# Two-block transformer kernel: up and gate tiles in pairs as seven block products of 256 tokens, and the down projection in chunks of four tiles between them

## The reference

```
first block:   h2 = rms_norm(x, norm_mlp)
               x  = x + square(relu(h2 @ w_up)) @ w_down          # 1024 -> 4096 -> 1024
second block, 2 layers, each with two of these around its mixer:
               h  = rms_norm(x, norm)
               x  = x + 0.5 * ((silu(h @ w_gate) * (h @ w_up)) @ w_down)   # 1024 -> 2816 -> 1024
out = rms_norm(x, final_norm)
```

## Time and profile before

| | |
|---|---|
| median of 3 runs | 2491.19 us |
| profiled execution | span 2488.4 us, PE busy 2471.6 us (99%) |
| DVE, ACT, POOL busy | 1235.0, 961.9, 198.7 us |
| matmuls | 11236 |

### The profile page before, as it was taken

How to read it: one execution, slowest core, us unless ns; L and a number is a source line. 1 busy time by engine, 2 the same in 40 slices (tenths; PEclk the granted TensorE clock), 3 DMA queues, 4 the chain that set the end, 5 groups by cost and what they waited for, 6 DMA issues and landing times.

```text
span 2488.4 us, 27808 instructions
## 1 busy us (share of the span) xinstructions
PE 2471.6 (99%) x11236; PEld 2046.0 (82%) x11236; DVE 1235.0 (50%) x1674; ACT 961.9 (39%) x1415; POOL 198.7 (8%) x207
## 2 busy tenths in 40 slices
PE   9999999999999999999999999999999999999999
PEld 7878888888888888888888888888888888888887
DVE  7742554434474343466554444643444665544443
ACT  6677343322443232357432222422222575322223
POOL 2231010000020000012200000100000122000001
PEclk9999999999999999999999999999999999999999
DMA  7655433333233333245433332333332364333332
GB/s 212 141 129 124 136 102 103 95 100 101 85 94 101 102 93 95 86 134 143 119 94 102 93 101 86 102 95 100 93 102 81 123 142 129 94 102 93 102 91 79
DMA packets 79279, 267.40 MB, mean 107 GB/s; under 512 B 9904, under 2 KB 13232, under 8 KB 78768
## 3 DMA queue, kind: packets, MB, share of 16 engines
q1 hardware_dynamic: 69376, 233.57, 31.0%
q0 software_dynamic: 9776, 32.06, 6.4%
HBM read 234.56 MB, written 2.19 MB: 95 GB/s over the span
## 4 chain that ended last, share of the span: by engine, by line
PE 90%; DVE 3%; issue 2%; ACT 2%; POOL 1%; DMA 1%; SPq 0%; POOLq 0%; DVEq 0%; ACTq 0%
PE bank L845 29%; PE bank L847 29%; PE bank L846 29%; DVE w_lo L1237 1%; PE bank L861 1%; PE bank L876 1%; ACT w_hi L1006 1%; DVE x L1367 1%; PE bank L899 1%; ACT z L994 0%; PE bank L888 0%; PE bank L889 0%; ACT h_hi L1019 0%; POOL rel_bias L1561 0%; POOL square_sum L1542 0%
## 5 line engine op out<-in xcount | busy, mean ns | idle before, releaser
L845 PE MATMUL bank<-h_hi,w_hi 128*128 128x512 f32 x2224 | 872.4, 392 | 3.6 <-DVE w_lo L1237 1.5
L846 PE MATMUL bank<-h_lo,w_hi 128*128 128x512 f32 x2224 | 866.6, 390 | 0.0
L847 PE MATMUL bank<-h_hi,w_lo 128*128 128x512 f32 x2224 | 866.4, 390 | 0.0
L1237 DVE TENSOR_TENSOR w_lo<-w_raw,w_hi 128x1024 fp32r<-128x1024 f32 (+2 forms) x392 | 484.0, 1236 | 289.8 <-ACT w_hi L1006 288.6
L1006 ACT ACTIVATE w_hi<-w_raw 128x1024 fp32r<-128x1024 f32 (+1 forms) x435 | 449.1, 1034 | 398.7 <-PE bank L847 396.5
L845 PEld LDWEIGHTS bank<-h_hi,w_hi 128*128 128x128 f32 x2224 | 417.7, 188 | 88.0 <-DVE h_lo L1252 2.7
L847 PEld LDWEIGHTS bank<-h_hi,w_lo 128*128 128x128 f32 x2224 | 417.5, 188 | 88.0
L846 PEld LDWEIGHTS bank<-h_lo,w_hi 128*128 128x128 f32 x2224 | 417.9, 188 | 81.9 <-issue 0.5
L845 PE MATMUL bank<-act_hi,w_hi 128*128 128x512 f32 x960 | 373.6, 389 | 0.0
L846 PE MATMUL bank<-act_lo,w_hi 128*128 128x512 f32 x960 | 373.6, 389 | 0.0
L847 PE MATMUL bank<-act_hi,w_lo 128*128 128x512 f32 x960 | 373.6, 389 | 0.0
(11 more groups left out here) (203 smaller groups left out, 1724.8 us busy)
## 6 DMA issues: line engine op xcount, KB each, us to landing
w_raw<-ffn_wg_dram SPq DMA_DIRECT2D x88, 512.0 KB, 3.5
w_raw<-ffn_wu_dram SPq DMA_DIRECT2D x88, 512.0 KB, 3.5
w_raw<-w_in_dram SPq DMA_DIRECT2D x67, 512.0 KB, 3.6
w_raw<-ffn_wd_dram SPq DMA_DIRECT2D x64, 512.0 KB, 3.5
w_lo<-w_raw POOLq DMA_DIRECT2D x51, 512.0 KB, 4.5
w_raw<-w_up_dram SPq DMA_DIRECT2D x32, 512.0 KB, 3.5
w_raw<-w_down_dram SPq DMA_DIRECT2D x32, 512.0 KB, 3.7
w_raw<-w_out_dram SPq DMA_DIRECT2D x24, 512.0 KB, 3.6
```

What stands on the lines that cost most here:

```text
L845: engine.matmul(to, w_hi[s][:, lhs], hi, start=k == 0, stop=False)
L846: engine.matmul(to, w_hi[s][:, lhs], lo, start=False, stop=False)
L847: product = engine.matmul(to, w_lo[s][:, lhs], hi, start=False, stop=job == "k_last")
L1237: engine.tensor_tensor(lo, value, hi.bitcast(F32), ALU.subtract).then_inc(signals[event].s, 1)
```

## The change

**Products.** Two hidden tiles (256 weight columns) make a group. Weights, `h` and result are cut into 2 by 2 blocks: even and odd channel tiles, the two hidden tiles, and the first and second 256 tokens. Winograd's form of Strassen's scheme then needs seven block products of 4 k-steps instead of eight: 84 matmuls of 256 columns where two hidden tiles took 48 of 512. There are 16 groups in stage 1 and 22 (gate and up by turns) in each of the other four, 104 in all.

**What the scheme adds.** Four sums of weight blocks per group (`s_t13`, `s_t2`, `s_t4` on DVE), so that seven blocks instead of four are split in hi and lo (`s_hi` on ACT, `s_lo` on DVE). Four sums of blocks of `h`, once per stage (`hs_tile`, `h_mix`). Sums of the products: some are added up in PSUM, others are copied out first (`s_copy` on ACT, four times 256 columns), and DVE adds them (`s_c22`, `s_sum`) and scales (`s_gate`, `s_up`, `s_relu`, `s_rescale`).

**Order.** Chunks are four hidden tiles (the first of a 22-tile MLP two), and the k-steps of a chunk's down projection are laid between the products of later groups (`fill`, `quota`): eight steps per group in the MLPs with gates, sixteen in stage 1, none in the first three groups of a stage and, with gates, four in the next four. Group n+1 is prepared during group n, with two slot buffers; the first two of a stage during the stage before. In the MLPs `w_lo` of a unit is now written to a buffer of its own, two slots after `w_hi`.

The core of the diff:

```diff
+HALF = TOKENS // 2
+HALF_K = KT // 2
+SLOT = HALF_K * P
+CHUNKS_FF = {FF1_TILES: (4,) * 8, FF2_TILES: (2, 4, 4, 4, 4, 4)}
...
+PART_OF = {B11: "first", T1: "first", B22: "last", T3: "last", T2: "mixed", T4: "mixed", B21: "b21"}
+PRODUCTS = {"P1": (B11, "a11", "x"), "P2": (B21, "a12", "y"), "P3": (B22, "s4", "x"), "P4": (T4, "a22", "z"),
+            "P5": (T1, "s1", "x"), "P6": (T2, "s2", "x"), "P7": (T3, "s3", "z")}
+STEADY = ("P1", "P7", "P6", "P4", "P5", "P2", "P3")
+OPENING = ("P1", "P2", "P4", "P6", "P7", "P5", "P3")
+COPY_AFTER = {"P1": "p1", "P6": "u1", "P5": "u3"}
+COPY_BEFORE = {"P6": "p1", "P5": "u1", "P3": "u3"}
...
+    def prepare(self, n, slots=8):
+        assert n == self.prepared
+        self.prepared += 1
+        for after, job, key in ((0, "s_t13", (n,)), (1, "s_t2", (n,)), (1, "s_hi", (n, "first")), (2, "s_t4", (n,)),
+                                (2, "s_hi", (n, "last")), (3, "s_lo", (n, "first")), (4, "s_hi", (n, "mixed")), (5, "s_lo", (n, "last")),
+                                (6, "s_hi", (n, "b21")), (7, "s_lo", (n, "mixed")), (9, "s_lo", (n, "b21"))):
+            self.later(slots + after, job, *key)
+
...
+    def strassen(self, g):
+        group = self.sg[g]
+        assert self.prepared > g
+        if self.prepared == g + 1 and g + 1 < self.block_end:
+            self.prepare(g + 1)
+        quota, passed = self.quota, 0
+        used = ("s_out", g + 1) if group.kind == "gate" else ("act_lo", (group.stage, group.pair))
+        for name in group.order:
+            for k in range(HALF_K):
+                if k < HALF_K - 1:
+                    self.add("s_step", (g, name, k))
+                else:
+                    self.add("s_last", (g, name))
+                if k % 2 == 1:
+                    self.next_slot()
+            if name in COPY_AFTER:
+                self.add("s_copy", (g, COPY_AFTER[name]))
+            if name == ("P4" if group.opens else "P7"):
+                self.add("s_copy", (g, "q4" if group.opens else "p7"))
+            if name == "P5":
+                self.sz2[g] = self.z(*used)
+                self.add("s_c22_open" if group.opens else "s_c22", g)
+            if name == ("P7" if group.opens else "P2"):
+                self.sz1[g] = self.z(*used)
+                self.add("s_sum", g)
+            if name == "P6":
+                self.load("a", g + 2)
+                if group.opens:
+                    self.norm(self.pending_norm)
+                    self.pending_norm = None
+            passed += 1
+            self.fill(quota * passed // 7 - quota * (passed - 1) // 7)
+        self.load("b", g + 2)
+        self.grouped()
+
...
+    def grouped(self):
+        if self.waiting:
+            self.filling += self.waiting
+            self.waiting = []
+            self.quota = -(-len(self.filling) // self.quota_over)
...
+    def hidden_pair(self, s, pair):
+        g = self.groups_done
+        for t in (2 * pair, 2 * pair + 1):
+            self.hidden[s, t] = t
+        if s == 1:
+            self.strassen(g)
+            self.later(1, "s_relu", g)
+            self.later(3, "s_square", g)
+            self.groups_done += 1
+        else:
+            self.strassen(g)
+            self.later(1, "s_gate", g)
+            self.later(3, "s_silu", g)
+            self.later(6, "s_rescale", g)
+            self.strassen(g + 1)
+            self.later(1, "s_up", g + 1)
+            self.groups_done += 2
+        self.group_of[s, pair] = self.groups_done - 1
+        self.later(5 if s == 1 else 3, "s_act", s, pair)
+        self.later(7 if s == 1 else 5, "s_act_lo", s, pair)
...
     def mlp(self, s, n_tiles):
         self.phase_result[s] = len(self.results) - 1
-        sizes = [min(FF_CHUNK, n_tiles - start) for start in range(0, n_tiles, FF_CHUNK)]
-        made = 0
-        for c, size in enumerate(sizes):
-            start = c * FF_CHUNK
-            until = start + size + (c + 1 < len(sizes))
-            while made < until:
-                self.hidden_tile(s, made)
-                made += 1
-            source, last = ("act", s, start), c == len(sizes) - 1
-            results = self.dense_pair(size, source) if last else []
-            for m in range(KT):
...
-                if last and s == FINAL - 1:
-                    self.output_norm_tile(m)
-                elif last:
-                    self.norm_tile(s + 1, m)
-            self.hidden_until += [r] * size
+        self.split_job = "split_late"
+        start = 0
+        chunks = chunk_units(n_tiles)
+        self.quota = 0
+        for c, (start, size, units) in enumerate(chunks):
+            last = c == len(chunks) - 1
+            for pair in range(start // 2, (start + size) // 2):
...
+                        if name == "P1" and g >= 2:
+                            pe.wait_ge(*done("s_out", g - 2))
+                        if name == ("P2" if group.opens else "P7") and g >= 2:
+                            pe.wait_ge(*done("s_summed", g - 2))
+                            pe.wait_ge(*done("s_c22", g - 2))
+                        if name in COPY_BEFORE:
+                            pe.wait_ge(*done("s_copied", (g, COPY_BEFORE[name])))
+                        if name == ("P7" if group.opens else "P4"):
...
+                    opens = k == 0 and name in ("P1", "P2", "P4" if group.opens else "P7")
+                    closes = job == "s_last" and name in ("P3", "P2", "P7" if group.opens else "P4")
+                    engine.matmul(to, slot_hi[:, g % 2, slot, lhs], hi, start=opens, stop=False, skip_group_check=True)
+                    engine.matmul(to, slot_hi[:, g % 2, slot, lhs], lo, start=False, stop=False, skip_group_check=True)
+                    product = engine.matmul(to, slot_lo[:, g % 2, slot, lhs], hi, start=False, stop=closes, skip_group_check=True)
+                    if job == "s_last":
+                        product.then_inc(signals["s_mm"].s, 1)
...
+                elif job == "h_mix":
+                    s, j = key
+                    act.wait_ge(*done("mix_31", key))
+                    engine.activation(h_hi[:, 2 * j, second_half], h_mixed[:, 0, :], ACT.Copy)
+                    act.wait_ge(*done("mix_4", key))
+                    engine.activation(hs_hi[:, :, j, :], h_mixed[:, 1:4, :], ACT.Copy).then_inc(signals["mix_hi"].s, 1)
...
+                elif job == "s_copy":
+                    g, what = key
+                    product = {"p1": "P1", "u1": "P6", "u3": "P5", "p7": "P7", "q4": "P4"}[what]
+                    act.wait_ge(*done("s_mm", (g, product)))
+                    if what in ("p1", "u1"):
+                        to, src = part_a[:, first_half if what == "p1" else second_half], x_bank[g % 2][:, first_half]
+                        if g > 0:
+                            act.wait_ge(*done("s_summed", g - 1))
...
+                elif job == "h_mix":
+                    s, j = key
+                    v.wait_ge(*done("h_full", (s, 2 * j + 1)))
+                    if j > 0:
+                        v.wait_ge(*done("mix_hi", (s, j - 1)))
+                    engine.tensor_tensor(h_mixed[:, 0:2, :], h_quarters[:, 0:4:3, :], h_quarters[:, 1:2, :].broadcast_to([P, 2, HALF]),
+                                         ALU.subtract).then_inc(signals["mix_31"].s, 1)
+                    v.wait_ge(*done("mix_31", key))
+                    engine.scalar_tensor_tensor(h_mixed[:, 2, :], h_quarters[:, 0, :], -1.0, h_mixed[:, 1, :],
+                                                ALU.mult, ALU.subtract).then_inc(signals["mix_2"].s, 1)
+                    v.wait_ge(*done("mix_2", key))
+                    engine.scalar_tensor_tensor(h_mixed[:, 3, :], h_mixed[:, 2, :], -1.0, h_quarters[:, 2, :],
...
+                elif job == "s_t13":
+                    n = key
+                    v.wait_ge(a_landed[n % 2].s, 16 * (n // 2 + 1))
+                    v.wait_ge(b_landed[n % 2].s, 16 * (n // 2 + 1))
+                    if n >= 2:
+                        v.wait_ge(*done("s_mm", (n - 2, "P5")))
+                        v.wait_ge(*done("s_mm", (n - 2, "P7")))
+                    engine.tensor_tensor(slot_raw[:, n % 2, T1:T3 + 1:T3 - T1, :], slot_raw[:, n % 2, B11:B22 + 1:B22 - B11, :],
+                                         slot_raw[:, n % 2, B12:B12 + 1, :].broadcast_to([P, 2, SLOT]), ALU.add).then_inc(signals["s_t13"].s, 1)
...
+                elif job == "s_sum":
+                    group = plan.sg[key]
+                    v.wait_ge(*done("s_copied", (key, "u1")))
+                    v.wait_ge(*done("s_mm", (key, "P7" if group.opens else "P2")))
+                    engine.tensor_tensor(buffer(plan.sz1[key]), yz_bank[key % 2][:, :], part_a[:, :], ALU.add).then_inc(signals["s_summed"].s, 1)
+
+                elif job in ("s_gate", "s_up"):
+                    s, (z1, z2) = plan.sg[key].stage, zs_of(key)
+                    by_1, by_2 = (rms_inv, neg_rms) if job == "s_gate" else zs_of(key - 1)
+                    if job == "s_gate":
```

(14 more changed lines are left out.)

470 lines of the change are left out of this document (353 added, 117 removed).

## The result

The changed kernel takes 2599.39 us, the median of 4 runs (2598.11 to 2600.92), against 2491.35 for the kernel before in the same job: 1.0436 times as long, 95% interval 1.0421 to 1.0451. The forecast was 2435, in a range of 2378 to 2482.

A forecast was written before the change was run, and what follows sets the result against it. PE's matmuls, count times pace, were taken as the bound. To 2488.4 us: products -117.3, groups without down steps +31, starts +10, mixing h +20, giving 2432.1; with 2.8 for the median, 2435, range 2378 to 2482.

The forecast's parts named there:

- The price of a product: In the up and gate groups, a 256-column product costs PE 116 ns, so PE gains 117.3 us.
- rival (e): On PE, the skill's gap rule holds for products: PE gains 179 us, giving 2373 us; chance 0.03.
- Mixing h: At stage starts, making sums of h blocks and their high and low parts costs 20 us (5 to 45).
- POOL: Between two MLPs, POOL's sums hold up DVE's mixing; 7 us taken for 4 to 5, 11 for 1 to 2.
- Groups without down steps and the reciprocal: Early groups with few or no down steps cost 31 us (0 to 45); reciprocal at five starts 10 (0 to 20).
- Filled groups: In groups with eight down steps, PE's loop of 15.2 us leads DVE's 14.1 by 1.1 us.
- Both signs of being wrong: In the profile after: filled groups taking more than 15.3 us, or products standing 120 ns apart or more.
- Rival (d): DVE's loop of 16.0 us bounds the filled groups, so the kernel is slower at 2529 us; chance 0.09.
- DVE's busy time: Over the whole kernel, DVE's busy time rises by about 750 us to 2000, above 80% of the span.
- copies: On ACT, four copies of products per group, about 0.43 us each, costed at nothing in filled groups.
- transfers: Weight fetches carry the same bytes and land 3.5 us after their slot is free; costed at nothing.

The follow-up runs named there:

- e3: The changed kernel with 370 matmuls on constants into an idle bank in front of PE's long waits at the starts; 2593.45 us.
- e1: The kernel before, with each 512-column matmul in the MLPs' up and gate steps cut into two of 256 columns; 2557.54 us.
- e2: The changed kernel without mixing of h, its products reading plain blocks of h instead; 2516.62 us.
- e4: The changed kernel with the same instructions, but each engine's part of a stage start, and the units' high and low parts, put further on in the queues; 2575.37 us.
- e8: e4's kernel with plain products in the first two groups of each stage and the last pair's mixing beside the first group; 2536.36 us.
- e6: The changed kernel with POOL adding one column of each square instead of 512; 2570.45 us.
- e5: The changed kernel with each stage's second group prepared during its first instead of before it; 2595.94 us.
- e7: e4's kernel with each stage's second group prepared during its first instead of before it; 2595.08 us.

## Why the prediction was wrong

The span rose by 110.7 us (2488.4 to 2599.1). Products give -82.4, PE's added idle time +124.7, and what remains, 68.4, is wider spacing of matmuls. By the trace some 40 of it lie in stretches at 1.2 GHz: 208 products there stood 226 ns apart and 83 matmuls of 512 columns 444. e3 showed that this is hardly a cause of its own, since PE would have stood instead. So all that is not the products' own pace costs 193, where the forecast had 61.

- **The price of a product** was read as 116 ns, from single pairs 0.11 and 0.12 apart; it is 120, and the gain 82 instead of 117. A term mis-sized by 35 us, and inside the bounds that were given (82.4 at 120). The step behind it was wrong too: the cost over the columns' own time was taken to shrink, while every matmul carries the same part, 13.2 ns in e1. The earlier trace rows hold that already: 226.5 less 512 columns at 2.4 GHz, 213.3, leaves 13.2, and 106.7 + 13.2 is 119.9. The Trainium skill (TensorE: Matmul & The Clock Gate, section Back-to-back issue gap) gives N/2.4 + 2.5 ns for an isolated matmul, an estimate of 109 ns for 256 columns; the same run has 120, so that figure and rival (e) fail here.
- **Mixing h**, 20 us in the forecast, is the step that failed. It says that "only the chain behind the last tile shows", three times 2 us after out projections, by setting 6.0 us of DVE work for a pair against 10.9 on PE. It left out what else stands in the same queue in that stretch: the second of a pair's two units (1.2 us), the preparation of two groups (6.9 each), POOL's share, and the time DVE stands for ACT. The trace has 42.0 of work and 22 of standing against PE's 38.1. Waits for `h_lo` and `w_raw_lo` are 90.6 us, and the three starts after an out projection, priced lowest, show the longest ones (9.1 and 7.8). e2 (83 us with mixing gone, 42 us of waits left), e4 (24 for the order, net) and e8 (39 more, with load ahead of the first product taken away) say that amount and handovers act together.
- **POOL** was seen as a price between two MLPs only. A sum is there in every start, at every tile but the first: e6 gives 29 us.
- **Groups without down steps and the reciprocal** were 31 + 10. The waits for `part_a` and `part_b`, 27.2 us, are what the trace shows for them: the size is right within the range. By the order of ACT's and DVE's lists the copies stand behind `s_sum` and the preparation; no run tests that apart.
- **Filled groups**: PE leads, as forecast, at 15.6 us instead of 15.2, with no waiting inside the window shown. Both signs of being wrong that the prediction named, products 120 ns apart and filled groups above 15.3 us, came true, through the price of a product alone. Rival (d), DVE's loop as the bound of filled groups, which carried most of the slower side, did not happen. The slower result came from a place that the rivals didn't name.
- **DVE's busy time**, forecast near 2000, is 1871; copies took 0.38 us instead of 0.43, and transfers land in 3.9 us instead of 3.5, without a wait of PE for them that matters.
- **The clock** had no place in the working. It was at 1.2 GHz at the end of the waits of 8 and 9 us, longer than any that the working had. e3 took away most of the time at 1.2 GHz, and 5.9 us came back.

Still open: how much of each start is amount and how much is handover. e4 cut handovers e5 and e7 amount, and what one gives depends on the other and on the place the work goes to. That the new layout of the down chunks alone would cost anything was not tried apart.

## What to carry to other kernels

Before costing a scheme that lightens the main engine, add up every helper's queue over the stretch where the scheme starts, with all that stands in it already and with every handover in it, and compare that sum with the main engine's time there; the average busy share (50% before) says nothing on it. Where two in-order engines pass one chain back and forth, put each one's part where its input is already there. An order that helps where a tile takes eight slots can hurt where it takes four, as e4 shows: look at each kind of start by itself. Price a matmul of half the columns from the steady pace of long ones, as columns' time plus a fixed part, and not from single pairs; e1 is such a test.

## What the hardware showed that was not expected

Each fp32r matmul with its own weight load cost its columns at 2.4 GHz plus 13.2 ns: 226.5 ns at 512 columns, 120 at 256 (e1). After a wait of 9.1 us PE's products stood 0.21 apart, the clock of 1.2 GHz, from 1310 to 1324 us in stage 4's start, though it was working most of that time; filling such waits with constant matmuls lifted the mean clock from 0.972 to 0.994 and gave 5.9 us (e3). A DVE sum of 0.69 us with both inputs in SBUF took 1.75 beside a POOL sum of 1.32, the same at all 20 places of the changed kernel.
